# A conditioning vector taken by row products on VectorE instead of column sums on three engines, in a fused decoder block

## What is computed

```python
mod = silu(c) @ ada_w + ada_b                    # c: 1024, ada_w: 1024 x 6144
sh1, sc1, g1, sh2, sc2, g2 = split(mod, 6)
h = rms_norm(x, norm1_g) * (1.0 + sc1) + sh1
x = x + g1 * token_mixer(h, ...)                 # projections, attention branches, merge, w_out
h = rms_norm(x, norm2_g) * (1.0 + sc2) + sh2
x = x + g2 * peer_ffn(h, ...)                    # 128 of 16384 experts per token, gathered
return rms_norm(x, final_g)
```

## Time and profile before

| | us |
|---|---|
| three runs | 933.20, 931.22, 930.38 |
| median | 931.22 |
| the profiled execution, its own time | 930.88 |
| its span, first to last instruction | 929.1 |
| busy in the span: TensorE / VectorE / ScalarE / GpSimd | 775.1 / 654.0 / 413.7 / 285.8 |
| bytes read, mean rate over the span | 340.65 MB, 368 GB/s |
| mean granted clock of TensorE, share of full speed | 0.98 |

### The profile page before, as it was taken

The page is one execution under the profiler, slowest core; times in us unless marked ns, Lnnn a source line. Parts: engine busy times, 40 slices in busy tenths (PEclk is TensorE's granted clock), DMA queues, the critical chain, the costliest instruction groups (busy, mean ns, idle before and its releaser), DMA issues.

```text
span 929.1 us, 9674 instructions
## 1 busy us (share of the span) xinstructions
PE 775.1 (83%) x2880; PEld 418.6 (45%) x2880; DVE 654.0 (70%) x1697; ACT 413.7 (45%) x1157; POOL 285.8 (31%) x262
## 2 busy tenths in 40 slices
PE   4999999998978897897787798778687777877785
PEld 3445778888724453354444364323222222222221
DVE  4534669974798879867666868685966757576656
ACT  3112222342568789342424543564634344353433
POOL 0000000000444344553333445525354252543430
PEclk8999999999999999999999999999899999999999
DMA  9967249660799999999999999999999999999993
GB/s 362 423 260 328 91 158 378 279 273 23 284 423 420 420 393 393 424 420 417 419 420 419 420 418 423 420 422 421 421 424 420 422 422 420 422 420 423 422 420 152
DMA packets 47619, 342.33 MB, mean 368 GB/s; under 512 B 5392, under 2 KB 6608, under 8 KB 11088
## 3 DMA queue, kind: packets, MB, share of 16 engines
q0 software_dynamic: 37152, 268.45, 69.8%
q1 hardware_dynamic: 9968, 72.79, 19.6%
q10 hardware_dynamic: 448, 0.48, 0.2%
HBM read 340.65 MB, written 1.05 MB: 368 GB/s over the span
## 4 chain that ended last, share of the span: by engine, by line
DMA 44%; PE 30%; DVE 13%; ACT 4%; issue 4%; POOL 3%; SPq 0%; POOLq 0%; DVEq 0%
DMA extra<-in_uv,arena 27%; DMA arena<-in_uv,arena 13%; PE banks L808 7%; PE banks L562 6%; PE banks L516 5%; DVE extra L1711 3%; PE banks L525 3%; POOL extra L929 3%; DMA extra<-in_uv,last_rows 2%; PE banks L778 2%; PE banks L759 2%; DMA extra<-in_w_ada 2%; PE banks L747 2%; DVE arena L1711 1%; DVE arena L1730 1%
## 5 line engine op out<-in xcount | busy, mean ns | idle before, releaser
L929 POOL DMA_INDIRECT extra<-in_uv,arena x132 | 150.1, 1137 | 430.2 <-DVE arena L1759 236.9
L808 PE MATMUL banks<-extra 128*128 128x512 f32 x472 | 231.4, 619 | 58.7 <-ACT extra L1169 57.7
L808 PE MATMUL banks<-arena,extra 128*128 128x512 f32 x312 | 156.3, 626 | 40.6 <-ACT extra L1169 40.6
L1156 ACT ACTIVATE arena<-arena 128x1 f32<-128x1 f32 x256 | 51.6, 202 | 305.3 <-DVE arena L1711 304.8
L808 PEld LDWEIGHTS banks<-extra 128*128 128x128 f32 x472 | 82.4, 191 | 184.2 <-ACT extra L1169 114.0
L929 POOL DMA_INDIRECT arena<-in_uv,arena x84 | 93.9, 1118 | 135.3 <-PE banks L808 58.5
L1711 DVE CUSTOM_DVE_ANT_0 extra<-extra 128x1024 f32<-128x1024 f32 x75 | 91.6, 1225 | 36.4 <-DMA extra<-in_uv,arena 35.2
L808 PEld LDWEIGHTS banks<-arena,extra 128*128 128x128 f32 x312 | 54.5, 192 | 130.4 <-ACT extra L1169 84.9
L1711 DVE CUSTOM_DVE_ANT_0 extra<-extra,arena 128x1024 f32<-128x1024 f32 x59 | 72.2, 1225 | 43.7 <-DMA extra<-in_uv,arena 43.1
L1169 ACT ACTIVATE extra<-tab,arena 128x128 f32<-128x128 f32 x234 | 93.9, 401 | 7.7
L808 PE MATMUL banks<-ring,extra 128*128 128x512 f32 x152 | 74.4, 616 | 20.6 <-ACT extra L1169 20.4
(11 more groups left out here) (280 smaller groups left out, 1044.7 us busy)
## 6 DMA issues: line engine op xcount, KB each, us to landing
arena<-in_w_ada SPq DMA_DIRECT2D x6, 2048.0 KB, 8.4
arena<-in_w_late SPq DMA_DIRECT2D x24, 512.0 KB, 8.2
extra<-in_w_ada SPq DMA_DIRECT2D x6, 1024.0 KB, 17.1
extra<-in_w_gate SPq DMA_DIRECT2D x3, 2048.0 KB, 8.3
extra<-in_w_in SPq DMA_DIRECT2D x2, 2048.0 KB, 31.6
extra<-in_w_ada SPq DMA_DIRECT2D x2, 2048.0 KB, 9.8
extra<-in_w_br SPq DMA_DIRECT2D x2, 2048.0 KB, 9.2
arena<-in_w_wq SPq DMA_DIRECT2D x2, 2048.0 KB, 14.5
```

Source lines behind the costliest of these rows:

```text
L808: last = nc.tensor.matmul(acc[tt][:, half * 512:(half + 1) * 512], diag[i % DIAGS], uv_slot[SLOT[v]][:, D + half * 512:D + (half + 1) * 51 ...
L929: nc.gpsimd.indirect_dma_start(uv_slot[SLOT[g]], None, A["uv"], bass.IndirectOffsetOnAxis(ap=expert[:, g:g + 1], axis=0)).then_inc(uv_in[S ...
L1156: link(nc.scalar.activation(gel[:, v:v + 1], dots[:, v:v + 1], ACT.Gelu))
```

## The change

The weight is transposed on the host: a row of 1024 belongs to one output of the vector and lies along one partition, and silu(c) lies as a row of 1024 on every partition. One VectorE instruction, a product with its sum along the row (`condition`), gives 128 outputs and puts them straight on the partitions; it writes its products over the weights. TensorE's `ada`, the partial sums and ScalarE's part are gone. silu(c) comes from c copied to 128 rows (0.5 MB), one sigmoid on ScalarE and one product on VectorE.

The first section is loaded in eight pieces of 1 MB (two rows per partition: shift and scale of one k tile), with the first weights in four parts behind pieces 0, 3, 5 and 7. Each k tile is modulated and projected by itself; the last two are projected together. The table of the root is loaded by a small operation behind the squares; the constant tables and small weights are issued from ScalarE behind the first shift. Chunks 4 to 11 are 2 MB as before, now four row products each: chunk 4 ahead of the fifth rope, chunk 5 behind the sixth, chunk 6 in two halves (behind the last rope, among the score sums), chunks 7 to 11 in the units. The load list and the buffers are reordered for it. The cut diff:

```diff
-FIRST_PARTS = ((0, 2), (2, 4), (4, KT))
-LOADS = [("ada", 0), ("ada", 1), ("ada", 2), ("ada", 3)] + [("win", m) for m in range(FIRST, len(CHUNKS))]
...
+FIRST_PARTS = tuple((k, k + 2) for k in range(0, KT, 2))
+LOADS = [("win", 3), ("win", 4), ("ada", 4), ("ada", 5), ("ada", 6), ("gate", 0), ("gate", 1), ("ada", 7), ("gate", 2),
+         ("ada", 8), ("ada", 9), ("gate", 3), ("ada", 10), ("ada", 11), ("wq", 0), ("br", 1), ("br", 0), ("out", 0),
+         ("out", 1), ("wq", 1)]
...
+IN_UNITS = [(m, c) for m in range(7, 12) for c in range(4)]
+UNIT_ADA = [IN_UNITS[u * len(IN_UNITS) // EACH:(u + 1) * len(IN_UNITS) // EACH] for u in range(EACH)]
...
+            for k in range(KT):
+                sp.dma_start(ada1_piece(k), A["w_ada1"][k]).then_inc(ada1_in[k], 16)
+                for j in {0: (0,), 3: (1,), 5: (2,), 7: (3,)}.get(k, ()):
+                    lo, hi = (FIRST_COLS * i for i in FIRST_PARTS[j])
+                    sp.dma_start(arena[:, lo:hi], A["w_first"][:, lo:hi]).then_inc(first_in[j], 16)
...
-            ada(0)
...
+            for k in range(KT - 2):
+                if k % 2 == 0:
+                    pe.wait_ge(first_in[k // 2], 16)
+                for c in range(FIRST):
+                    project_rows(c, (k,))
+            pe.wait_ge(first_in[KT // 2 - 1], 16)
+            for c in range(FIRST):
+                project_rows(c, (KT - 2, KT - 1))
...
-                if u in ADA_AT:
-                    ada(ADA_AT[u])
...
+            act.dma_start(s_row, A["c"]).then_inc(c_in, 16)
+            act.wait_ge(const_set, 1)
+            nc.scalar.activation(small[:, 10:11], eps[:, 0:1], ACT.Sigmoid)
+            act.wait_ge(c_in, 16)
+            nc.scalar.activation(sigmoid, s_row, ACT.Sigmoid).then_inc(sig_ready, 1)
             act.wait_ge(x_in, 16)
             for k in range(KT):
                 nc.scalar.activation(sq1[:, k, :], x3[:, k, :], ACT.Square).then_inc(sq_ready, 1)
...
+            nc.scalar.activation(small[:, 11:12], eps[:, 0:1], ACT.Sqrt)
             act.wait_ge(ssq_ready, 1)
             nc.scalar.activation(rstd[:, :], B[0][:, 0:T], ACT.Sqrt, bias=eps[:, 0:1], scale=1.0 / D).then_inc(root_ready, 1)
...
+            for k in range(KT):
+                act.wait_ge(x_scaled, k + 1)
+                nc.scalar.activation(hT[:, k, :], hT[:, k, :], ACT.Identity, bias=mod[:, k:k + 1]).then_inc(h_ready, 1)
+                if k == 0:
+                    act.dma_start(tab[:, :], A["tab"]).then_inc(tab_in, 16)
+                    act.dma_start(wukv, A["w_ukv"]).then_inc(w2_in, 16)
+                    act.dma_start(w2kv, A["cmp_w2"]).then_inc(w2_in, 16)
+                    act.dma_start(posT, A["cmp_pos"]).then_inc(w2_in, 16)
...
+            V.tensor_tensor(s_row, s_row, sigmoid, ALU.mult).then_inc(s_ready, 1)
+
+            def condition(w, j):
+
+                V.tensor_tensor_reduce(out=w, in0=w, in1=s_row, scale=1.0, scalar=0.0, op0=ALU.mult, op1=ALU.add,
+                                       accum_out=mod[:, j:j + 1]).then_inc(ada_read, 1)
+
+            def ada(m, c):
+
+                condition(chunk(dve, "ada", m)[:, c * D:(c + 1) * D], 4 * m + c)
+
+            dve.wait_ge(s_ready, 1)
+            for k in range(KT):
+                dve.wait_ge(ada1_in[k], 16)
+                for i in range(2):
+                    condition(ada1_piece(k)[:, i * D:(i + 1) * D], i * KT + k)
+                if k == 0:
+                    dve.wait_ge(par_in, 16)
+                    dve.wait_ge(root_ready, 1)
+                    link(V.reciprocal(rstd[:, :], rstd[:, :]))
...
+                V.scalar_tensor_tensor(hT[:, k, :], x3[:, k, :], s1, rstd[:, :], ALU.mult, ALU.mult).then_inc(x_scaled, 1)
...
+            for c in range(4):
+                ada(4, c)
             for r in range(4, 8):
                 rope(r)
+                if r == 5:
+                    for c in range(4):
+                        ada(5, c)
...
             for r in range(8, len(ROPES)):
                 rope(r)
+            for c in range(2):
+                ada(6, c)
...
             for q in range(4):
                 score_add(q)
+                if q % 2 == 0:
+                    ada(6, 2 + q // 2)
...
-                for m, k in UNIT_ADA[u]:
-                    ada_step(m, k)
+                for m, c in UNIT_ADA[u]:
+                    ada(m, c)
...
-            dve.wait_ge(ada_done, 12)
+            dve.wait_ge(ada_read, 6 * KT)
```

More of the change, by code:

```diff
@@ L348, in build @@
         w1v = ring[:, 1024:2048].rearrange("p (l e) -> p l e", l=CMP_LEN // 2)
-        ada_sum += [ring[:, 2048 + i * 512:2048 + (i + 1) * 512] for i in range(2)]
+        s_row = ring[:, 2048:3072]
+        sigmoid = scr[:, 0:1024]
         ssb = [ring[:, i * 512:(i + 1) * 512] for i in range(2)]
@@ L440, in _ @@
                     sp.wait_ge(z_done, 2 * FIRST)
-                elif BEFORE[n] is not None:
+                elif BEFORE[n] is None:
+                    sp.wait_ge(ada_read, 4 * ADA1_SLOTS.index(SLOT_OF[n]) + 4)
+                else:
                     old, i = LOADS[BEFORE[n]]
-                    sp.wait_ge(*{"ada": (ada_summed, i + 1), "win": (z_done, 2 * i + 2), "gate": (fill_done, 4 * i + 4)}[old])
+                    sp.wait_ge(*{"ada": (ada_read, 4 * i + 4), "win": (z_done, 2 * i + 2), "gate": (fill_done, 4 * i + 4)}[old])
                 slot = wslot[SLOT_OF[n]]
@@ L482, in _ @@
         def _(pe):
-            def ada(m):
-                pe.wait_ge(ada_summed, m + 1)
-                if m < 4:
-                    for c in range(4):
-                        last = nc.tensor.matmul(B[6 + m % 2][:, 4 * m + c:4 * m + c + 1], ada_part[m % 2][0][:, c * P:(c + 1) * P],
-                                                ones[:, 0:1], start=True, stop=True)
-                    last.then_inc(ada_done, 1)
-                    return
-                for c in range(4):
-                    last = nc.tensor.matmul(B[7][:, 4 * m + c:4 * m + c + 1], ada_buffer(m, 0)[:, c * P:(c + 1) * P],
-                                            ones[:, 0:1], start=True, stop=True)
-                last.then_inc(ada_done, 1)
             def square_sum(bank, src, ready, done):
@@ L1293, in ada_rest @@
-            def ada_rest(m):
-                dve.wait_ge(ada_in[m], 16)
-                w = wslot[SLOT_OF[CHUNK_NO["ada", m]]].rearrange("p (k n) -> p k n", k=KT)
-                for k in range(2, KT):
-                    if k == 4:
-                        chunk(dve, "ada", m)
-                    part = ada_part[m % 2][k % 2]
-                    if k < 4:
-                        dve.wait_ge(ada_first, 2 * m + k - 1)
-                    else:
-                        dve.wait_ge(dve_step, summed[m, k - 2])
-                    ins = V.scalar_tensor_tensor(part, w[:, k, :], silu[:, k:k + 1], part, ALU.mult, ALU.add)
-                    ins.then_inc(dve_step, 1)
-                    steps[0] += 1
-                    summed[m, k] = steps[0]
-                dve.wait_ge(dve_step, steps[0])
-                parts = ada_part[m % 2]
-                V.tensor_tensor(parts[0], parts[0], parts[1], ALU.add).then_inc(ada_summed, 1)
@@ L1907 @@
     w_in = a["w_in"][0]
+    ada_rows = a["ada_w"][0].T.reshape(6 * KT, P, D)
     def columns(n):
```

157 lines of the change are left out of this document (30 added, 127 removed).

## The result

The kernel after takes 918.46 us in the median (916.31 to 922.34), the kernel before 930.80 in the runs made beside it: a ratio of 0.9872, with an interval of 0.983 to 0.9914. The forecast was 919.6, range 916.0 to 924.5. The profiled execution took 917.91 us (span 916.1), 12.97 less than that of before. When it was run once more (six runs) the ratio was 0.9878 (0.9855 to 0.9900).

The account below looks back on a forecast made before the run. The first gather's start, set by TensorE's program order, was taken as the bound; 2.5 + 2.4 + 4.6 + 2.3 - 0.2 = 11.6 us off the profiled 930.88 gave 919.3, forecast as a 919.6 median, range 916.0 to 924.5.

Parts of the forecast that it names:

- Bound by the start of the gathers: Whole kernel: TensorE's program order sets the first gather; time taken out before 237 us comes off the end whole.
- Start of the projections, 2.5: First section: the first projection starts at 18.7 instead of 21.24 us; gain 2.5 us, bounds 1.2 and 2.6.
- 18.91 - 1.28: First section: with the 1.28 us table load moved behind the squares, the first product starts at 17.63 instead of 18.91 us.
- Pace of the projections, 2.4: First section: three groups of ones-matmuls of 0.79 us each leave TensorE and nothing else waits; gain 2.4 us.
- The clock rival: First projections: TensorE's clock stays low for longer after idle time, costing 3.4 us, so 923.0 us; chance 0.09.
- Insertions, 0: Among the ropes and score sums: VectorE's inserted products fit into its idle gaps; no loss, at most 2.45 plus 1 us.
- The two thin covers: First the fifth rope's wait for TensorE, second the copy among the score sums: each hides its inserted products with 0.3 us spare.
- Units, 4.6: Attention units, third to twelfth gate: without the ones-matmul groups gates follow every 4.81 us, 43.3 instead of 47.9; gain 4.6 us.
- about 52: First twelve attention units: VectorE's load falls from 58.6 to about 52 us, below TensorE's 57.7.
- Tail, 2.3: Last gate's start to the turn of the outputs: 7.0 us instead of 9.3; gain 2.3 us.
- ScalarE's lag, -0.2: After the units: ScalarE, which opens the gates in that time, then lags by 0.2 us, a loss.
- The slower rival: All stages: a row product takes twice its time (2.45 us), net 8.6 us slower, 939.8 us; chance 0.04.

Follow-up runs that it names:

- the first fillers: Kernel after plus unread matmuls of ones on TensorE, twenty ahead of the square sums and eighteen between these and the first projection: 915.21 us, ratio to before 0.9845.

## Why the prediction was right

The four terms reckoned at 2.5, 2.4, 4.6 and 2.3 us measured 2.45, 2.49, 4.58 and 2.06: 11.6 of the 13.0 us. The rest lies in the square sums and the last stretch, for which the sum had no term, and in the turn, where it had -0.2 and 0.36 came.

*Bound by the start of the gathers.* Right: the first gather starts 12.7 us earlier and the span ends 13.0 earlier.

*Start of the projections, 2.5.* The size was right (2.45 from the end of the square sums to the first projection), the reason for half of it was not. Of the 2.45 us 1.3 lie ahead of the reciprocal, which starts 0.59 us behind the square sums instead of 1.89, and 1.2 between the first product and the first shift (0.52 instead of 1.70; 0.45 was reckoned). But the step "18.91 - 1.28" priced the table load as if it alone held the reciprocal; moved by itself it gave nothing. It is the load together with VectorE's sum of the first conditioning piece that went; the sum alone was not tried. A further 0.71 us of the start was not forecast, and the spread of the square sums given above leaves it to luck. c landed at 4.53, ahead of x, as assumed. In the kernel after the table load ends at 12.11 (10.83, 1.28 long) and the next operation of ScalarE starts at 12.12. The drain that the Trainium skill adds to a load (ScalarE: Activation LUTs, section "What ACT_TABLE_LOAD costs") is not in this trace.

*Pace of the projections, 2.4.* Right (2.49), with the clock low for about as long as before. The clock rival fell, but it named the right place: filled, the stretch takes 40.59 us, so the low clock costs 1.7 to 2.5 us in the three executions of the new stretch (42.28, 42.28 and 43.06 us), and 3.0 with the groups put back. In the five of the old one it costs 1.8 to 3.3, if the three groups are taken off too (44.77 to 46.22 us). That the change lengthens it does not show. TensorE: Matmul & The Clock Gate (section "Part 1: The HAM clock gate") of the Trainium skill says that the number of slow matmuls differs from run to run of one kernel; the spread of these executions agrees.

*Insertions, 0.* Right in these two executions, and in part by luck. Row products last 1.22 us in every stage (median 1220, 1217 to 1227 ns over all 48), and the stretch among the ropes is as long as before. The two thin covers kept 0.81 and 0.5 us, where 0.3 was reckoned. But the second cover was read in a trace whose gate ahead of it took 5.34 us and kept in one where it took 5.41; where that gate takes 3.72, as in the runs with the groups back and with the first fillers, it is 1.16 us short.

*Units, 4.6.* Right to 0.02 us, with a reason that was half of the matter: TensorE's order does set the pace, but cutting the groups alone left the time where it was. VectorE's load was mis-sized: "about 52" us were reckoned, 41.84 measured. The old work took 42.9 us in that stage (31.05 for the steps with two inputs, 7.03 for those with one, 4.84 for the sums, lines 1284, 1282 and 1290), within the bounds given; 58.6 - 42.9 + 24.5 is 40.2. The sum did not hang on it, since both lie below TensorE's 57.7.

*Tail, 2.3, and ScalarE's lag, -0.2.* 2.06 and +0.36; the lag did not come, and the turn itself took 0.66 + 0.60 us instead of 1.12 + 1.06. In the kernel before with only VectorE's steps cut it took 0.66 + 0.60 too; what decides it was not tried.

*The slower rival* had the right sign and places, and its sum broke on the end of the first section, as shown.

## What to carry to other kernels

Where two engines are both over 95% busy in a stage, price a change by what it leaves on each; cutting one alone can measure as nothing, and that is no proof that the cut was worthless. A cover of a few tenths of a microsecond holds only as long as nothing ahead of it gets faster, so work inserted into a gap belongs where the slack is large. Where TensorE idles shortly ahead of dense work, matmuls that nobody reads can pay for themselves: the two places in the first section gave 2.2 to 2.5 us here, and with a third in the second norm and the waits behind them moved it was 4 to 5.

## What was not expected of the hardware

In these kernels ScalarE's table load was not held by the wait of the operation that needs it when that was the only wait ahead of it (10.68 against 14.73 us, and 12.27 against 15.18), and was held when a second one stood there (14.93); this rests on three kernels, and why it is so was not tried. The gate at 104 us of the kernel after runs at the low clock (5.41 us, granted clock 0.56 and 0.59 in the windows of 104 to 108), though the longest idle time of TensorE between the first projection and it is 1.41 us. In other executions the same gate takes 3.72, behind the same 1.41 us: so with the groups put back, and with the first fillers. What decides this was not settled. The clock column reads 1.00 up to 18 us in the kernel after, while its square sums run at 0.70 of the rate they reach with fillers (3.72 against 5.31 us); at the start of this program the duration of the matmuls tells more than that column.
